# Expert weight slabs that wait for the landing of the slab two places ahead

## What is computed

```python
def swiglu(h, wg, wu, wd):
    return (jax.nn.silu(h @ wg) * (h @ wu)) @ wd
# per token: the 2 best of 8 experts by the router's logits, softmax over the two,
# and the weighted sum of swiglu(h, wg[e], wu[e], wd[e]); wg, wu: 1024 x 2816, wd: 2816 x 1024
```

## Time and profile before

| what | us |
|---|---|
| executions without profile, median (3) | 1563.74 |
| the profiled execution's own time | 1569.43 |
| its span, from the first to the last instruction | 1567.7 |
| expert passes on TensorE, from about 745 to 1555 in the span | about 810 |
| TensorE's mean granted clock, share of full | 0.986 |

### The profile page before, as it was taken

The page is one execution under the profiler, slowest core; times in us unless marked ns, Lnnn a source line. Parts: engine busy times, 40 slices in busy tenths (PEclk is TensorE's granted clock), DMA queues, the critical chain, the costliest instruction groups (busy, mean ns, idle before and its releaser), DMA issues.

```text
span 1567.7 us, 44059 instructions
## 1 busy us (share of the span) xinstructions
PE 1461.3 (93%) x20574; PEld 1212.6 (77%) x20574; DVE 282.6 (18%) x705; ACT 203.5 (13%) x530; POOL 130.3 (8%) x200
## 2 busy tenths in 40 slices
PE   6999999999999999999999889997899988888987
PEld 5667666666666667767998889997799978888986
DVE  2354720000000245464100000000000000000012
ACT  1245410000000024532000000000000000000000
POOL 3221116000000011111100000000000000000010
PEclk9999999999999999999999999999999999999999
DMA  9933338993323523342899999999999999999991
GB/s 249 254 114 106 110 112 286 364 320 127 123 82 119 137 85 91 95 132 94 285 396 379 360 366 349 346 340 352 349 352 361 383 352 364 334 358 346 355 375 62
DMA packets 197689, 398.49 MB, mean 254 GB/s; under 512 B 11922, under 2 KB 67866, under 8 KB 197344
## 3 DMA queue, kind: packets, MB, share of 16 engines
q1 hardware_dynamic: 180720, 346.38, 64.3%
q0 software_dynamic: 15216, 46.34, 9.3%
q10 hardware_dynamic: 1568, 2.91, 0.7%
HBM read 360.00 MB, written 37.57 MB: 254 GB/s over the span
## 4 chain that ended last, share of the span: by engine, by line
PE 91%; issue 5%; DVE 2%; DMA 1%; ACT 0%; SPq 0%; ACTq 0%; DVEq 0%
PE bank L1328 30%; PE bank L1350 15%; PE bank L1233 13%; PE bank L784 7%; PE bank L1250 6%; PE bank L767 2%; PE bank L1097 2%; PE bank L1080 2%; PE bank L753 1%; PE bank L1052 1%; PE bank L1064 1%; PE bank L738 1%; PE bank L707 1%; DMA arena<-in_x_sample 1%; PE bank L1364 1%
## 5 line engine op out<-in xcount | busy, mean ns | idle before, releaser
L1328 PE MATMUL bank<-arena,ring 128*64 128x108 f32 (+7 forms) x11264 | 478.2, 247 | 51.7 <-issue 51.4
L1328 PEld LDWEIGHTS bank<-arena,ring 128*64 128x64 f32 x11264 | 467.9, 138 | 62.0 <-issue 61.1
L1350 PE MATMUL bank<-arena,ring 128*64 128x108 f32 (+7 forms) x5632 | 242.4, 249 | 27.5 <-issue 27.5
L1350 PEld LDWEIGHTS bank<-arena,ring 128*64 128x64 f32 x5632 | 236.9, 140 | 32.1 <-issue 31.9
L1233 PE MATMUL bank<-hnT,ring 128*128 128x336 f32 x704 | 199.1, 446 | 1.8 <-DVE hnT L1712 1.8
L1233 PEld LDWEIGHTS bank<-hnT,ring 128*128 128x128 f32 x704 | 133.8, 190 | 67.1 <-issue 2.3
L784 PE MATMUL bank<-hnT,ring 128*128 128x336 f32 x384 | 120.1, 458 | 0.0
L2195 DVE TENSOR_TENSOR arena<-arena,bank 128x432 f32<-128x432 f32 (+15 forms) x48 | 24.6, 513 | 469.5 <-PE bank L1328 469.4
L1250 PE MATMUL bank<-arena,ring 128*128 128x336 f32 x352 | 99.6, 446 | 0.0
L784 PEld LDWEIGHTS bank<-hnT,ring 128*128 128x128 f32 x384 | 70.8, 193 | 35.0 <-issue 7.0
L1250 PEld LDWEIGHTS bank<-arena,ring 128*128 128x128 f32 x352 | 67.0, 190 | 32.5
(11 more groups left out here) (387 smaller groups left out, 1071.2 us busy)
## 6 DMA issues: line engine op xcount, KB each, us to landing
ring<-in_moe_w_gate SPq DMA_DIRECT2D x88, 1024.0 KB, 7.6
ring<-in_moe_w_up SPq DMA_DIRECT2D x88, 1024.0 KB, 7.5
ring<-in_moe_w_down SPq DMA_DIRECT2D x88, 1024.0 KB, 6.8
ring<-in_w_in SPq DMA_DIRECT2D x16, 1024.0 KB, 6.8
ring<-in_w_gate SPq DMA_DIRECT2D x11, 1024.0 KB, 10.4
ring<-in_w_up SPq DMA_DIRECT2D x11, 1024.0 KB, 15.8
xg_rows<-arena POOLq DMA_DIRECT2D x1, 11200.0 KB, 48.5
y_rows<-arena POOLq DMA_DIRECT2D x1, 11200.0 KB, 89.4
```

What stands on the lines that cost most here:

```text
L1328: ins = mm(into[part, rows * fi:rows * fi + rows], weights[:, c, col:col + 64], xg[:, k0 + c, :], start=(k0 + c == 0 and fi == 0), stop=(k ...
L1350: ins = mm(bank[5 + c // 4][part, rows * (c % 4):rows * (c % 4) + rows], weights[:, col:col + 64], hid[:, f, :], start=(f == 0 and c % 4 = ...
```

## The change

SP gets one more wait ahead of each expert slab of the eight main passes. Before slab j of expert k is issued, SP waits until the slab two places earlier has landed, in this expert or the one before. The first two slabs of the first expert have no such wait. The branch for crowded experts keeps the old form. Nothing else is touched.

```diff
-            def expert_slabs(k, e, rows_at):
+            def expert_slabs(k, e, rows_at, ahead=False):
                 for j in range(FFN_SLABS):
                     if j == 18 and rows_at is not None:
                         expert_rows(k, rows_at)
                     s = (MOE0 + j) % RING
                     sp.wait_ge(slab_free, k * FFN_SLABS + (MOE0 + j - RING + 1))
+                    if ahead and (k or j >= 2):
+                        k2, j2 = (k, j - 2) if j >= 2 else (k - 1, j - 2 + FFN_SLABS)
+                        s2 = (MOE0 + j2) % RING
+                        sp.wait_ge(slab_here[s2], k2 * (16 * FFN_SLABS // RING) + fixed_seen[s2] + 16 * (j2 // RING + 1))
...
-                expert_slabs(k, e, RANK_AT[k + 1] if k < EXPERTS - 1 else None)
+                expert_slabs(k, e, RANK_AT[k + 1] if k < EXPERTS - 1 else None, ahead=True)
```

## The result

The changed kernel took 1600.32 us (median of 4 executions, 1593.90 to 1605.54) against 1565.54 us before (4 executions), a ratio of 1.0211 with a 95% interval of 1.0179 to 1.0244. The medians are 34.8 us apart. The forecast was 1555 us and the range ended at 1599. The profiled execution took 1593.90 us, the fastest of the four, and its span is 1592.2 us. All rows after are read against that span.

What follows compares the result with a forecast made beforehand. TensorE's program refills, slowed by slab traffic, bound the kernel; afterwards slab supply would. 779.8 + 727.7 + 30 + 5.8 + 2.7 + 12.8 = 1558.8 us span, less 3.96: 1555 us, range 1505 to 1599.

Steps and rivals of the forecast that it cites:

- The 79 us of stalls: TensorE in the expert passes: 72 waits for its next packet of program, made slow by slab traffic; gain nothing to 79 us.
- The reserve: Last slab issued 33.8 us before the last product ends; the change would spend it down to 8.5 us.
- other traffic: Output stores, gathers and `xg_rows` loads in the slabs' DMA engines from slab 18 on: 23 to 40 us, taken as 30.
- the supply: Slab delivery with two in flight, said to become the bound: 3.09 us per slab on average against 3.03 before.
- rival A: Slower: each program refill hits every slab pair in full, spacing 3.11 us, 1593 us in the span, 1589 us; chance 0.30.
- P: Spacing per slab with two in flight, without other traffic: taken as 2.97 us, bounded by 2.58 and 3.11.
- Its counter-argument: Against rival A: packets of program served in the gap the loop itself leaves are free; no size given.
- break-even: The P at which the span stays unchanged, 3.006 us; above it rival A decides.
- Rival B: Much faster: two slabs in flight are enough, TensorE is the bound, a quarter of stalls left, 1505 us; chance 0.15.
- Rival C: No change: program refills come no sooner, TensorE keeps 3.03 us per slab and supply just keeps up, 1564 us; chance 0.13.
- One warning: Sign of being wrong: TensorE's idle time grows in the passes with many rows; no size given.
- the other warning: Sign of being wrong: DMA rate in the passes with many rows falls under 330 GB/s.

Runs made afterwards that it cites:

- half_steps: Kernel before, each slab issued as two half transfers, the first waiting for the slab three places ahead, the second two: 1545.61 us, ratio 0.9866.
- half the program: Every second block of the experts' products left out, all slabs still loaded: 1502.83 us on the kernel before, 1573.17 us on the changed one.
- The reduced traffic: Six `xg_rows` loads and seven `y_rows` stores cut from 112 to 16 rows: changed kernel 1565.66 us, kernel before 1543.40 us.
- mix: Two-place wait kept only for slabs issued while TensorE is in passes of 90 rows or fewer, elsewhere as before: 1559.58 us, ratio 0.9963.

## Why the prediction was wrong, point by point

**What bounds the kernel before: right in the main.** The 79 us of stalls were by program and came with the refills, 82 to 84 us with three, four and eight places. That the slabs' depth makes them is shown by `half_steps`: 60.7 us with not one wait for a slab, and 20.3 us less time. The 8.9 us with two places and 0.7 with one do not show it, since TensorE's waits for slabs cover the refills there. Uncovered, two places took the stalls from 10.6 to 7.8 us (848 to 905 us). So two places took off far less of the 79 us than the fall to 8.9 suggests, as far as this one stretch tells.

**The reserve is spent: right.** From 33.8 us to 9.6, forecast 8.5 from the last issue's landing and last slab. The terms of the span, one by one:

| term | forecast | measured |
|---|---|---|
| issue of slab 18 | 779.8 | 780.2 |
| 245 slabs, with other traffic | 727.7 + 30 = 757.7 (3.09 each) | 789.3 (3.222 each) |
| landing of the last | 5.8 | 6.5 |
| its products | 2.7 | 3.1 |
| to the end | 12.8 | 13.1 |
| span | 1558.8 | 1592.2 |

**The step that failed** is the supply, 31.6 of the 33.4 us. The form (landing and a little, over two) was right, and rival A was the case that came, at 1593 in the span against 1592.2, with its P of 3.11 and my 30 of other traffic where the chip had 3.01 and 50: its sum came out, its parts did not, so that it came so close is luck. The larger part of the miss is the other traffic, 20 us, and P has 9. Both were read where the loop was not closed. P was read off a line through two stretches in which SP did not wait for a landing. There a slab that is held up delays nobody: its successors are in the queue already. With two places a late landing is a late issue, and then the engines run dry. The trace shows this. In a stretch of 32 us in the first pass, 794 to 826 us, eleven down slabs are issued. The one at 797.2 lands after 5.0 us, and this is the next, with its landing:

```profile
L491 SPq DMA_DIRECT2D ring<-in_moe_w_down x1: 367/367/367, 799.8 to 799.8; - x1
...
DMA to landing us min/median/max: 6.4/6.4/6.4
```

The slab after, at 802.3, took 6.5, and the next ones 5.1 and 5.1, then 6.5 and 6.6: landings 2.5 to 2.7 us apart, and every fourth 3.9 or 4.0. So one hold-up of 1.3 us passes through both slabs in flight. What the engines moved around the late landing at 799.8 + 6.4 = 806.2, in the columns of the earlier trace rows:

```profile
804.80:806.20 1.40, 1.40 (x36) 1.40 (x34) 0.60 (x1) 0.00 (x0) 0.00 (x0) 1.00 1.02 421
806.20:807.60 1.40, 1.40 (x36) 1.40 (x33) 0.00 (x0) 0.00 (x0) 0.00 (x0) 1.00 0.83 205
```

421 GB/s just before it and 205 in the 1.4 us after: the next slab is issued at 806.2, and its bytes are not moving yet. Rival A said it in words: a packet on one engine holds up the landing, the landing the next issue, and fifteen engines idle.

Its counter-argument came true in part: a packet served in the gap that the loop leaves costs little or nothing. One packet of program crosses from 801.7 to 802.7 us, ahead of the late landing. The next crosses from 806.6 to 807.7, in the gap behind that landing, and the landings after it are 2.6 and 2.5 us apart. The engines beside these two packets, same columns:

```profile
801.60:802.80 1.20, 1.20 (x31) 1.20 (x29) 0.00 (x0) 0.00 (x0) 0.00 (x0) 1.00 1.01 399
806.50:807.70 1.20, 1.20 (x31) 1.20 (x29) 0.00 (x0) 0.00 (x0) 0.00 (x0) 1.00 0.73 140
```

Counted over the 93 refills away from other traffic: where slabs fill 95% of the engines or more (31 of them), the landing behind is 1.1 us late on average, and where they fill under 60% (22) it is 0.6 us. With half the program 42 of 45 refills meet engines filled to 85% or more, and these cost 1.25 us. This goes far to explain why a refill costs 0.8 us in the changed kernel and 1.2 to 1.3 us there.

I sorted the 245 intervals between landings. The 69 without a packet of program or other traffic lie 0.02 us above the 2.53 (down) and 2.64 us (gate and up) of undisturbed slabs. The 141 with a packet of program lie 0.65 to 0.73 above, about 99 us together, 0.8 per refill. The rest, near `xg_rows`, `y_rows` and the gathers, adds about 50. For this each interval is taken some 1.5 us ahead of its landing, since a packet crosses before the landing that it holds up. With 1.3 to 2.0 us instead, the program gets 92 to 99 us and the other traffic 48 to 56. Not moved at all, the intervals with and without a packet do not differ (0.50 and 0.47 us), so the split hangs on this step. So:

- **P** was (637 + 100) / 245 = 3.01 where I had 2.97: 9 us. With everything else as forecast, 3.01 would still have been a draw, by the break-even of 3.006.
- **Other traffic** was 50 where I had 30, and 40 as its end: 20 us. Each burst was priced by its size, 1.15 us, when the row of the landing behind it said 3.3. In a loop that follows landings, the landing is nearer to the price. The reduced traffic measured 28 to 35 us for thirteen bursts.

The sum by this sorting, 637 + 99 + 50 = 786 us, leaves 3 of the 789.3 unexplained.

**Rival B** (two in flight are enough) falls: no more than 68 us, the first stretch, look like it. **Rival C** falls by the spacing, 3.222 us where it had 3.03, and by SP's 249 waits. What it said of the refill, that it comes no sooner, is not refuted by the 8.9 us, which the waits for slabs cover.

**From the span to the median.** I took 3.96 us off, as the profiled execution before lay above the median. After, it is the fastest of four, and the median lies 8.1 us above its span. These 12 us carry the median past rival A's 1589 to 1600 and out of the range, 1.3 us above its end. Without them the time would still have been slower than before where faster was forecast.

**The chances.** Slower had 0.34. The break-even left P a margin of 0.036 us, a quarter of the width that I gave P (2.85 to 3.0), and the other traffic alone was unsure by 17 us, 0.07 per slab. For both terms the text named a row that pointed upward (slabs at 5.8 to 6.4 us beside engines with slack, 3.3 us behind an `xg_rows` load), and both were taken below it. That deserved more than 0.34.

**Signs in the profile.** The landing near 6 us (6.2) and its maximum under 14.8 (10.3), SP's waits ended by slabs, TensorE's new waits ahead of lines 1328 and 1350, and the last product within 10 us (9.6) all came. The stalls after 128 loads were not shorter where nothing covers them: 7.8 / 6 and 10.6 / 8 are both 1.3 us; there were fewer. The spacing of 3.2 or more with few stalls by program was named as the sign of A. One warning came true too: idle time in the pass of 112 rows grew from 1.5 to 4.3 us. GB/s there fell from 346 to 330, the edge of the other warning.

**The rule weighed.** The Trainium skill, Runtime: NRT & Kernel Launch, section Instruction fetch mechanics, says that crossing a block of program is mostly hidden. With three, four and eight places this kernel loses 82 to 84 us to it, so the trace goes on disagreeing. It is hidden once the slabs are in the earlier trace rows, and where TensorE waits for slabs anyway (0.7 us with one place and with half the program).

## What stays open

Why a refill holds up a landing by 1.3 us when its packet takes 1.07 us on its engine was not tried. How much of the stalls by program two places would take away if the supply kept up is open; only 57 us of one trace bear on it. Whether cover between 1 and 1.5 slabs, by unequal pieces, does better wasn't tried either. How much `mix` and `half_steps` would bring together is open.

## What to carry to other kernels

A limit on transfers in flight closes a loop in which every hold-up of a landing becomes a hold-up of supply. Before adding one, compare (mean landing, refills and bursts included, plus issue) / places with the spacing that the consumer needs, and price bursts by the landing behind them, not by their bytes. Do not take vanished stalls for a gain while another wait has come in their place: it may only cover them. Landing times read while the queue is open are too kind, since there nothing follows from a late one. If two places are too few and three are no limit at all, try a step in between: a transfer in two halves with different conditions gave 1.3% here, while two halves with the same condition cost 4%.

## What the hardware showed that was not expected

- The stalls by program do not scale with the depth while TensorE has slabs: 82 us with three places, 84 with eight, 61 with two and a half. The 9 us with two and 0.7 with one stand beside 84.5 and 479 us of waits for slabs, which cover them, just as with half the program and a queue of some six slabs (0.7 us).
- SP's issue instruction itself takes long when many slabs are queued: a median of 2.1 to 2.5 us and up to 10.3 us in the half-program kernel before, where landings take 16.1 us. With two places it is 0.37 us at the median and at most 0.46.
- 448 KB of other traffic costs 2.2 to 2.7 us with two places, about twice its share by size, and 1.7 to 2.0 us (22.5 to 26.0 us for thirteen bursts) where the slabs have a reserve.
- With TensorE at half the work, the deep queue supplied a slab per 2.85 us, 1,048,576 bytes / 2.85 us = 368 GB/s of slabs alone, and two places one per 3.17 us, 331 GB/s.
